# Router logits from x without its root, by halves of tokens, in a fused two-block transformer kernel

## The reference, cut to what matters

```python
x = x + merged @ w_out                     # the end of the mixer ("wout" in the kernel)
h = x * rsqrt(mean(x * x) + EPS) * ffn_g   # rmsnorm: one root a token, one gain a feature

def moe_ffn(h, router_w, w1, w3, w2):
    logits = (h @ router_w).astype(jnp.float32)
    top_vals, top_idx = lax.top_k(logits, TOP_K)          # TOP_K = 2 of N_EXPERTS = 8
    top_w = jax.nn.softmax(top_vals, axis=-1)
    gate = jnp.sum(jax.nn.one_hot(top_idx, N_EXPERTS, dtype=jnp.float32) * top_w[..., None], axis=-2)
    out = jnp.zeros_like(h)
    for e in range(N_EXPERTS):
        out = out + gate[..., e:e + 1].astype(h.dtype) * swiglu(h, w1[e], w3[e], w2[e])
    return out
```

## Time and profile before

| | us |
|---|---|
| median of 3 runs | 2172.72 (2171.02 to 2175.41) |
| the profiled execution's own time | 2175.5 |
| its span, first to last instruction | 2173.7 |
| TensorE busy | 2097.6 (96%) |
| VectorE busy | 1549.7 (71%) |
| ScalarE busy | 1189.9 (55%) |
| chain of work that ended last: PE, DVE, ACT | 91%, 5%, 2% of the span |

### The profile page before, as it was taken

One profiled execution on the slowest core, in us unless ns is written; L12 is line 12 of the kernel. 1 busy time (PEld: TensorE's weight loads), 2 busy tenths in 40 slices (PEclk: granted clock), 3 DMA queues, 4 the chain that ended last, 5 costly groups with the idle time before them and its releaser, 6 DMA issues.

```text
span 2173.7 us, 25628 instructions
## 1 busy us (share of the span) xinstructions
PE 2097.6 (96%) x10570; PEld 1716.2 (79%) x10570; DVE 1549.7 (71%) x1526; ACT 1189.9 (55%) x1258; POOL 52.7 (2%) x89
## 2 busy tenths in 40 slices
PE   7999999999999979999999999999978999999998
PEld 6877678887877768888888888888867788787887
DVE  5767766456767748999898989999866555566544
ACT  5544354446544337777777777777734444344443
POOL 0000000000000010000000000000010000000000
PEclk9999999999999989999999999999979999899999
DMA  8676665655667639999999999999953575424551
GB/s 308 238 257 228 236 231 183 206 170 194 252 233 255 249 126 329 357 363 366 347 366 365 355 356 365 367 365 367 370 177 98 166 244 192 145 92 142 193 193 59
DMA packets 370072, 549.04 MB, mean 253 GB/s; under 512 B 21271, under 2 KB 295575, under 8 KB 363031
## 3 DMA queue, kind: packets, MB, share of 16 engines
q1 hardware_dynamic: 365488, 536.53, 71.9%
q10 hardware_dynamic: 4460, 10.80, 1.5%
HBM read 546.13 MB, written 1.15 MB: 252 GB/s over the span
## 4 chain that ended last, share of the span: by engine, by line
PE 91%; DVE 5%; ACT 2%; issue 1%; POOL 0%; DMA 0%; DVEq 0%; SPq 0%; POOLq 0%; ACTq 0%
PE bank L441 85%; PE bank L469 2%; PE bank L528 2%; DVE wlo L1079 1%; ACT whi L1073 1%; DVE xn L1617 1%; DVE gate_tanh L1613 0%; PE bank L568 0%; PE bank L956 0%; DMA raw<-in_w_in 0%; PE bank L558 0%; DVE scoresB L1627 0%; PE bank L930 0%; PE bank L534 0%; DVE hTlo L1542 0%
## 5 line engine op out<-in xcount | busy, mean ns | idle before, releaser
L1079 DVE TENSOR_TENSOR wlo<-raw,whi 128x2048 fp32r<-128x2048 f32 x461 | 1051.2, 2285 | 386.2 <-ACT whi L1073 384.1
L1073 ACT ACTIVATE whi<-raw 128x2048 fp32r<-128x2048 f32 x461 | 881.4, 1913 | 458.2 <-PE bank L441 385.1
L441 PE MATMUL bank<-whi,hThi 128*128 128x512 f32 (+2 forms) x1104 | 439.2, 398 | 14.9 <-DVE hTlo L1542 8.1
L441 PE MATMUL bank<-whi,hTlo 128*128 128x512 f32 (+2 forms) x1104 | 431.1, 391 | 0.0
L441 PE MATMUL bank<-wlo,hThi 128*128 128x512 f32 (+2 forms) x1104 | 430.9, 390 | 0.0
L441 PEld LDWEIGHTS bank<-whi,hThi 128*128 128x128 f32 x1104 | 213.9, 194 | 82.6 <-issue 33.0
L441 PE MATMUL bank<-whi,slots_hi 128*128 128x512 f32 x704 | 275.2, 391 | 1.9 <-DVE slots_lo L1917 1.9
L441 PE MATMUL bank<-whi,slots_lo 128*128 128x512 f32 x704 | 274.8, 390 | 0.0
L441 PE MATMUL bank<-wlo,slots_hi 128*128 128x512 f32 x704 | 274.8, 390 | 0.0
L441 PEld LDWEIGHTS bank<-whi,hTlo 128*128 128x128 f32 x1104 | 214.0, 194 | 42.6
L441 PEld LDWEIGHTS bank<-wlo,hThi 128*128 128x128 f32 x1104 | 214.3, 194 | 40.0 <-issue 0.5
(11 more groups left out here) (304 smaller groups left out, 2247.8 us busy)
## 6 DMA issues: line engine op xcount, KB each, us to landing
raw<-in_moe_w SPq DMA_DIRECT2D x352, 512.0 KB, 6.0
raw<-in_moe_w SPq DMA_DIRECT2D x88, 1024.0 KB, 7.6
raw<-in_w_in SPq DMA_DIRECT2D x72, 1024.0 KB, 7.3
raw<-in_ada_w SPq DMA_DIRECT2D x48, 1024.0 KB, 7.1
raw<-in_ffn_w SPq DMA_DIRECT2D x44, 512.0 KB, 4.7
raw<-in_w_gate SPq DMA_DIRECT2D x44, 512.0 KB, 3.7
raw<-in_w_up SPq DMA_DIRECT2D x44, 512.0 KB, 4.7
raw<-in_w_down SPq DMA_DIRECT2D x22, 1024.0 KB, 4.8
```

What stands on the lines that cost most here:

```text
L441: m = mm(dst, l_, r_, start=start and i == 0, stop=stop and i == len(pairs) - 1)
L1073: s.then_inc(s.unit.activation(split_slot(whi, p)[:, 0:n], slot_of_ring(raw, p, NRAW)[:, 0:n], ACT.Copy), ("hi", p), sem="weights_hi")
L1079: e.then_inc(e.unit.tensor_tensor(split_slot(wlo, p)[:, 0:n], slot_of_ring(raw, p, NRAW)[:, 0:n], split_slot(whi, p)[:, 0:n].bitcast(F32), ...
```

## The change

The router's input is no longer the normed x but x times the gain. Leaving out the positive root of a token changes neither which two logits are largest nor their order; the difference of the two is multiplied with the root before the exponential, which is one more small instruction of VectorE.

- **The router by token halves.** `router_turn(l, 0)` stands ahead of the last twelve matmuls of `w_out`; `router_turn(l, 1)` behind the first half's logits. A half's eight blocks go to two banks: ScalarE evicts the first (`router_tokens`, four instructions), VectorE the second.
- **Weights.** In layer 1 `t.ahead` is 1 from the second token half of `w_out` on until the first gathers are issued. The split of the experts' second piece moves: on ScalarE behind x's high part, on VectorE behind the branch.
- **x's split by halves.** High part in two instructions of 1024 columns on ScalarE; low part of tokens 0 on GpSimd, of tokens 1 on VectorE while TensorE counts places.
- **First picks ahead of the branch.** `pick_slots(0)` builds the selection of the first two experts only, two instructions of 256 columns, ahead of the branch. The other pairs and the gates move between the first chunks of the first expert.
- **Four banks for the first gathers** (ring `high`), and `slots_ready` is told by halves of the features.

The diff, cut to its core (`t` is TensorE, `s` ScalarE, `v` VectorE, `g` GpSimd):

```diff
+            def router_turn(l, tt):
+                for k in range(0, KD, 4):
+                    t.wait_ge(("x_added", l, "mix", tt))
+                    bank = t.take(("router_h", tt, k))
+                    t.then_inc(transposes(bank, [x3[:, tt, (k + j) * P:(k + j + 1) * P] for j in range(4)]), ("full", ("router_h", tt, k)))
+
             def experts_router(l):
-                for k in range(0, KD, 2):
-                    t.wait_ge(("normed_x", l, "ffn", 0), ("normed_x", l, "ffn", 1))
-                    bank = t.take(("router_h", k))
-                    t.then_inc(transposes(bank, [xn3[:, tt, (k + j) * P:(k + j + 1) * P] for j in range(2) for tt in range(NT)]),
-                               ("full", ("router_h", k)))
                 bank = t.take("logits")
-                t.wait_ge("router_tokens")
                 for tt in range(NT):
-                    m = group(bank[:, tt * NE:(tt + 1) * NE],
-                              [(router3[:, k, pick_tokens(tt)], col("router", 0, k * NE, NE)) for k in range(KD)])
+                    if tt:
+                        router_turn(l, tt)
+                    for k in range(0, KD, 4):
+                        t.wait_ge(("router_tokens", tt, k))
+                        m = group(bank[:, tt * NE:(tt + 1) * NE], [(router3[:, k + j, pick_tokens(tt)], col("router", 0, (k + j) * NE, NE))
+                                                                   for j in range(4)], start=k == 0, stop=k > 0)
                 t.then_inc(m, ("full", "logits"))
...
             def dense_experts(l):
+                t.ahead = 1
...
                 def gather(pair, k):
-                    t.wait_ge("picked", "x_split")
-                    bank = t.take(("slots", pair, k), "top")
+                    t.wait_ge(("picked", pair), ("x_split", 0), ("x_split", 1))
+                    bank = t.take(("slots", pair, k), "top" if pair else "high")
...
                 def make_put(pair):
+                    t.wait_ge(("picked", pair))
                     bank = t.take(("put", pair), "top")
...
                     gather(0, k)
-                feed_forward("sparse", ("moe",), 1, nets_of(l), tokens, lambda e, tt, k: ("slots_ready", e // 2), "middle", "pair", between)
+                t.ahead = AHEAD
...
                 def turn_sum(tt, half):
-                    if tt and l % 2 == 0:
+                    if tt:
                         t.ahead = 1
                     if tt and half and l % 2 == 0:
                         features(x3, (l, "ffn"), lambda tt, k: ("x_added", l, "mix", tt), (0,), "high")
+                    elif tt and half:
+                        router_turn(l, 0)
...
+            def router_tokens(l, tt):
+                s.wait_ge(("full", ("router_h", tt, 0)))
+                for j in range(4):
+                    s.then_inc(act(router3[:, j, pick_tokens(tt)], s.bank(("router_h", tt, 0))[:, j * P:(j + 1) * P], ACT.Copy,
+                                   scale=col("ffn_g", l, j)), *([("free", ("router_h", tt, 0)), ("router_tokens", tt, 0)] if j == 3 else []))
...
                     square(x3, xn3, tt, 0, ("x_added", l, "mix", tt), ("squares", l, "ffn", tt))
+                    if l % 2:
+                        router_tokens(l, tt)
...
-                    s.wait_ge(("normed_x", l, "ffn", 0), ("normed_x", l, "ffn", 1))
-                    s.then_inc(act(hThi, xn, ACT.Copy), "x_hi")
+                    s.wait_ge(("full", (("wout", l, 1), 1)))
+                    for tt in range(NT):
+                        s.wait_ge(("normed_x", l, "ffn", tt))
+                        s.then_inc(act(xhi[:, tt], xn3[:, tt], ACT.Copy), ("x_hi", tt))
+                    s.split_ahead(("moe",), 2)
...
+            def router_tokens(l, tt):
+                v.wait_ge(("full", ("router_h", tt, 4)))
+                for j in range(4):
+                    v.then_inc(scalar(router3[:, 4 + j, pick_tokens(tt)], v.bank(("router_h", tt, 4))[:, j * P:(j + 1) * P],
+                                      col("ffn_g", l, 4 + j), None, ALU.mult),
+                               *([("free", ("router_h", tt, 4)), ("router_tokens", tt, 4)] if j == 3 else []))
+
+            def pick_slots(pair):
+                for tt in range(NT):
+                    e = tt * NE + 2 * pair
+                    v.then_inc(tensor(pick4[:, tt, 2 * pair:2 * pair + 2, :], rep(const("slots"), 2),
+                                      slot_of[:, e:e + 2].unsqueeze(2).broadcast_to([P, 2, P]), ALU.is_equal), *([("picked", pair)] if tt else []))
+
             def experts_router(l):
-                for k in range(0, KD, 2):
-                    v.wait_ge(("full", ("router_h", k)))
-                    for j in range(2):
-                        v.then_inc(scalar(router3[:, k + j, :], v.bank(("router_h", k))[:, j * T:(j + 1) * T], col("ffn_g", l, k + j), None, ALU.mult),
-                                   *([("free", ("router_h", k))] if j else []), *(["router_tokens"] if j and k == KD - 2 else []))
...
-                v.then_inc(tensor(w3_[:, :, 0], top3[:, :, 1], top3[:, :, 0], ALU.subtract), "weights_low")
+                v.then_inc(tensor(w3_[:, :, 1], top3[:, :, 1], top3[:, :, 0], ALU.subtract))
                 v.own()
+                v.then_inc(tensor(w3_[:, :, 0], w3_[:, :, 1], stat[:, 4:4 + NT], ALU.mult), "weights_low")
                 for tt in range(NT):
...
                 v.then_inc(tensor(taken8, first8, lg, ALU.add), "chosen")
+                v.wait_ge(("x_hi", 1))
+                v.then_inc(tensor(xlo[:, 1], xn3[:, 1], xhi[:, 1].bitcast(F32), ALU.subtract), ("x_split", 1))
...
                 v.then_inc(vcopy(flag[0:1, :], most[0:1, :]), "slots_known")
                 v.own()
+                pick_slots(0)
...
             def sparse_experts(l):
-                for tt in range(NT):
-                    v.then_inc(tensor(pick4[:, tt], rep(const("slots"), NE),
-                                      slot_of[:, tt * NE:(tt + 1) * NE].unsqueeze(2).broadcast_to([P, NE, P]), ALU.is_equal),
-                               *(["picked"] if tt else []))
-                gates()
-
                 def run(step):
                     if step is None:
                         return
-                    if step[0] == "gather":
+                    if step[0] == "put" and step[1] < NE // 2 - 1:
+                        if step[1]:
+                            pick_slots(step[1] + 1)
+                    elif step[0] == "put":
+                        gates()
...
-                                       *([("free", ("slots", pair, k))] if j else []), *([("slots_ready", pair)] if j and k == KD - 2 else []))
+                                       *([("free", ("slots", pair, k))] if j else []),
+                                       *([("slots_ready", pair, k - 2)] if j and k % 4 == 2 else []))
...
+                pick_slots(1)
...
+                    v.wait_ge(("row_out", *last_chunk[l]))
+                    router_tokens(l, 0)
                     scaled_by_root(l, "ffn", (0,))
                     add_to_x(l, "mix", lambda tt, hf: (("wout", l, hf), tt), [(1, 1)])
+                    router_tokens(l, 1)
                     scaled_by_root(l, "ffn", (1,))
-                    v.wait_ge(("row_out", *last_chunk[l]))
                     experts_router(l)
...
-                    g.wait_ge("x_hi")
-                    g.then_inc(tensor(hTlo, xn, hThi.bitcast(F32), ALU.subtract), "x_split")
+                    g.wait_ge(("x_hi", 0))
+                    g.then_inc(tensor(xlo[:, 0], xn3[:, 0], xhi[:, 0].bitcast(F32), ALU.subtract), ("x_split", 0))
```

More of the change, by code:

```diff
@@ L875, in sparse_experts @@
                     gather(0, k)
-                feed_forward("sparse", ("moe",), 1, nets_of(l), tokens, lambda e, tt, k: ("slots_ready", e // 2), "middle", "pair", between)
+                t.ahead = AHEAD
+                feed_forward("sparse", ("moe",), 1, nets_of(l), tokens, lambda e, tt, k: ("slots_ready", e // 2, k), "middle", "pair", between)
                 for step in behind_chunks:
@@ L1379, in dense_experts @@
             def dense_experts(l):
-                s.wait_ge("x_split")
+                s.wait_ge(("x_split", 0), ("x_split", 1))
                 features("dense", lambda k: col("ffn_g", l, k))
@@ L1480, in scalar_program @@
                                "weights_exp")
-                    s.wait_ge("slots_known", "x_split", ("mod_out", 0))
+                    s.wait_ge("slots_known", ("x_split", 0), ("x_split", 1), ("mod_out", 0))
                     load_shift_and_scale(0, 0)
@@ L1911, in run @@
                         return
-                    if step[0] == "gather":
+                    if step[0] == "put" and step[1] < NE // 2 - 1:
[3 more added lines that the diff above has]
+                        gates()
+                    elif step[0] == "gather":
                         _, pair, k = step
@@ L1944, in dense_experts @@
                 gates()
-                v.wait_ge("x_split")
```

(1 more changed line is left out.)

## The result

The kernel after takes 2158.38 us (median of four runs, 2157.92 to 2159.33), the one before on the same chip 2171.98 (2171.02 to 2175.41): a ratio of 0.9935, 95% interval 0.9923 to 0.9946, so 13.6 us less. The forecast was 2158.7, from 2155.0 to 2165.0. The profiled execution took 2157.9.

A forecast was written before the change was run, and what follows sets the result against it. The prediction took TensorE's idle, serial 30.8 us between `w_out` and the first expert as the bound. Gains of 13.05 + 1.7 less 0.3 and 0.4 made 14.05 us, so 2172.7 became 2158.7 us, range 2155.0 to 2165.0.

The forecast's parts named there:

- last add to x: Router's start: with the second piece's split moved away, the add follows the last `w_out` matmuls, 0.7 us earlier.
- logits: From x to the router's logits: norm off the path, half the work done beforehand; end 8.4 us earlier (7.8 to 9.0).
- flag: End of `most_tokens`, behind the router's small instructions: one added instruction costs 0.1 us, so it comes 8.3 us earlier.
- flag to gathers: From the flag to the first gather: two picks instead of all set the start, 2.2 us less.
- gathers to expert: First gather to first expert: 32 matmuls run through without waiting for banks, 2.5 us less (1.8 to 3.8).
- clock in the first expert: Behind the first expert's start: the half-clock stretch doesn't return once the stalls are gone, 1.7 us less.
- VectorE late in the expert stage: Picks and gates between first chunks cost 0.3 us (0 to 3.7); as rival all 3.7 show, 2162.0 us, chance 0.07.
- two small losses: Router: VectorE's handovers beside GpSimd's half, and a clock fall before 780 us, cost 0.4 us together.
- the first rival: Second half's logits, all gathers and 3.4 us of the first expert at half clock: 11 us gain, 2161.7, chance 0.16.
- The branch: Rival at the gathers' start: TensorE's branch cost, hidden under the picks, shows; 2.1 us at most, 2160.7, chance 0.07.
- The slower case: Rival in the first expert: the clock settles at the half and stays, 40 us giving 2178.7 us; chance 0.02.
- the gain at the router only: Rival: something outside the trace, like a late split, ties the gathers' start; 6 to 8 us gain, 2165.7, chance 0.05.

The follow-up runs named there:

- the two repeats: One more profiled run of each unaltered kernel: the changed one 2161.52 us (ratio 0.9941), the one before the change 2171.39 us.
- before again: The kernel before the change, run once more with nothing altered, to see its clock: 2171.39 us in one run.
- e4_root_only: Kernel before, with only the root left out: transposes read x, the root multiplies the difference of the two logits; 2173.39 us against 2172.70, ratio 1.0001.
- e5_four_banks_only: Kernel before, with only four banks for the first gathers, `slots_ready` still told for the whole pair; 2173.24 us against 2172.70, ratio 0.9998.
- e11_filler_on_before: Kernel before, with seventeen filler matmuls that nobody reads in the router's idle stretches; 2171.73 us against 2170.97, ratio 0.9995.
- after again: The changed kernel, run again with nothing altered as reference for its variants; 2161.52 us against 2173.34 for the kernel before, ratio 0.9941.
- e7_filler_light: Changed kernel plus five filler matmuls through the router into a bank nobody reads; 2155.23 us against 2172.70 for the kernel before, ratio 0.9915.
- e10_filler_two_banks: Changed kernel plus five filler matmuls, with the first gathers back on two banks; 2157.78 us against 2170.97 for the kernel before, ratio 0.9937.

## Why the prediction was right, step by step

The first column is the term as predicted, then the two profiles of the first chip, aligned at "0", and where it helps the two repeats.

| step | predicted | measured |
|---|---|---|
| `w_out` ends | +0.82 | +0.93 |
| last add to x | -0.7 | -0.57 |
| logits | -8.4 (7.8 to 9.0) | -8.56; repeats -7.2 |
| flag | -8.3 | -8.29; repeats -7.1 |
| flag to gathers | -2.2 | -2.28 |
| gathers to expert | -2.5 (1.8 to 3.8) | -2.66; repeats -2.2 |
| clock in the first expert | -1.7 | -1.70; repeats -0.1 |
| VectorE late in the expert stage | +0.3 | 0 |
| two small losses | +0.4 | inside the flag, 0.2 |
| sum | -14.05 | -14.9; repeats -11.7 |

**Right in mechanism and size.** The add starts at 774.87, within 0.1 us of the end of the last matmul's record (774.84), the logits end 5.5 behind it, the picks set the gathers' start (785.55, TensorE at 785.60), and the gathers run as one. The last `w_out` matmuls pay 0.87 us for eight transposes instead of 0.72.

**Mis-sized: the clock behind the expert's start.** I counted 1.7 us as sure, from one stretch at 808 to 812. From the expert's start to the first `put` the profile before has 7.18 us, but before again has 5.53, and `e4_root_only` and `e5_four_banks_only`, with the old router, 5.57 and 5.56; `e11_filler_on_before` has 7.16. After has 5.48. The stretch comes in some profiles of the old order and not in others, so the term should have been between 0 and 1.7. I also wrote that the stalls ahead of it brought it on; before again has the same stalls without it, so this cause is not shown.

**Wrong in attribution: the banks.** I gave the gathers' 2.5 us to 32 matmuls that run through instead of waiting for banks. Four banks are worth 0.1 to 0.3 us at the clock that the gathers then have, 0.65 to 0.84 in the old order. The size came out right since the wait for the whole pair's slots, which the prediction's sum had no price for, went at the same time: about 2 us by the trace of after, with no run of its own. This is luck in the size.

**Mis-sized without effect: VectorE ahead of the expert.** I put the gathers at 4.8 us at the earliest, with 0.65 us of VectorE's load and branch ahead of the second piece's split. With the clock held they take 4.09: the load stands between the two picks for 0.13 us and the split starts at 787.27, 0.15 us ahead of the first gather.

**The rivals.** The clock took part back in after again: its expert starts 1.4 us later. That is the mechanism of the first rival with about half of its price, since the clock is back before the expert (at 794.3, the expert at 794.81). That it can be held (`e7_filler_light`) shows 2.5 to 3.9 us there. The branch didn't come to light; TensorE's compare in after:

```profile
L1123 PEldq COMPARE_BRANCH  x2: 92/2626/5159, 785.3 to 1562.2; - x2
```

The short record is the one at the router, and the gathers start 0.05 us behind the picks, so of the up to 2.1 us nothing showed. The Trainium skill (Runtime: NRT & Kernel Launch, section "Instruction fetch mechanics") would have a stall only for a branch to a page that is not at hand; the short record, with the sparse way right behind the compare, agrees with that; the long one stands at the jump at the end, and no run shows what fills its 5.2 us. VectorE late in the expert stage cost nothing: from the first `put` to the end both kernels take 1359.1 to 1359.8. The slower case has no sign: the window 794 to 837 is at 1.00. Nor has the gain at the router only: no split and no part of x holds the gathers behind their picks.

**The total.** Between the first two profiles the span fell by 17.6 us: 14.9 up to the first `put`, 1.9 ahead of "0" and 0.7 behind the `put`. The last two belong to no edit. That the forecast of the median was right within 0.3 us is partly luck. It was taken from a median of before of 2172.7, which a fourth run made 2171.98, while the gain was 13.6 where 14.05 was forecast. Within the gain errors offset each other: 1.7 us of clock that before doesn't lose each time, against costs of 0.7 of which 0.2 came. The other chip gave 11.8 us (2173.34 to 2161.52), inside the range too, but nearer the first rival's 11 than the forecast's 14.05.

## What to carry to other kernels

A step taken off a serial path counts only if what is next is ready earlier too: in the old order the root gave nothing in its trace; with the halves, and the early turn that it allows there, about 3 us. Split the path so that its first half runs beside the work ahead of it, and then look at every instruction that stands between on each engine; one weight split at its old place made the last add 2.4 us later. Don't count as sure a stretch at the lower clock that one profile shows; take a second profile of the kernel before.

## What the hardware showed beyond that

**A small VectorE instruction that waits for GpSimd.** VectorE's and GpSimd's timelines in after, then in after again, then in `e7_filler_light`:

```profile
779.21 2.35 POOL L2284 TENSOR_TENSOR hTlo<-xn,hThi 128x1024 fp32r<-128x1024 f32 x1 [1.55 <-ACT hThi L1496]
...
781.22 0.38 DVE L1899 CAST small<-idx 128x16 f32<-128x16 uint32 x1
```

```profile
781.02 2.36 POOL L2284 TENSOR_TENSOR hTlo<-xn,hThi 128x1024 fp32r<-128x1024 f32 x1 [1.54 <-ACT hThi L1496]
...
784.05 0.18 DVE L1899 CAST small<-idx 128x16 f32<-128x16 uint32 x1
```

```profile
781.62 2.36 POOL L2291 TENSOR_TENSOR hTlo<-xn,hThi 128x1024 fp32r<-128x1024 f32 x1 [1.55 <-ACT hThi L1503]
...
783.53 0.49 DVE L1906 CAST small<-idx 128x16 f32<-128x16 uint32 x1
```

The change of type of 128x16 takes 0.18 us when GpSimd's subtraction is over (it ended at 783.38), and 0.38 and 0.49 when it is not: it ends at 781.60 and 784.02, 0.04 us behind GpSimd's 781.56 and 783.98. `e10_filler_two_banks` has it once more: 0.49 us, to 781.54, with GpSimd's to 781.50. The indices found beside the same subtraction (158 ns) are not slowed. The Trainium skill (SBUF — State Buffer, section "SBUF: two separate sides") says that the engine that comes second to the shared ports is blocked until the other's instruction is over, if VectorE's has two SBUF inputs or uses both ports. The end just behind GpSimd's agrees with that; this cast has one input, so it would have to be of the second kind. The price is 0.2 to 0.3 us where the prediction bounded it by 1.

**The clock and small matmuls.** In `e4_root_only` TensorE is busy for 6.68 of 7 us with records of 8 columns, and the granted clock is 0.55. With five matmuls of 256 columns more it stayed at 1.00 in one order; with seventeen it fell at 788.7 in the other, and TensorE was busy throughout the ten microseconds behind that. What keeps it up, and why, stays open.
